# A four-layer hybrid decoder trunk: the first loads in two chains, and products of zeros ahead of the first weights

## What is computed

```python
proj = x @ w_in[l]                        # columns: xa, gb, gc (384 each), p (256), u, v (384 each)
ya = gb * causal_conv3(gc * xa)
yb = (trailing_mean(p) - p) @ w_pool * pool_scale
u, v = gelu(u), gelu(v)                   # v: normalised in heads of 64
yc = u * (w_spatial_masked @ v + b_spatial)          # in chunks of 128 tokens
h = layer_norm(ALPHA * x + concat(ya, yb, yc) @ w_o)
x = layer_norm(ALPHA * h + (silu(h @ w_gate) * (h @ w_up)) @ w_down)
```

## Time and profile before

| | |
|---|---|
| time, median of 3 runs (lowest to highest) | 2626.9 us (2626.42 to 2627.59) |
| time of the profiled execution | 2631.07 us |
| its span on the slowest core (core 4) | 2629.5 us |
| spans of the eight cores in it | 2619.5 to 2629.5 us |
| PE busy | 2547.4 us, 97% |
| DVE, ACT, POOL busy | 1328.5, 745.0, 400.4 us |

### The profile page before, as it was taken

The page is one execution under the profiler, slowest core; times in us unless marked ns, Lnnn a source line. Parts: engine busy times, 40 slices in busy tenths (PEclk is TensorE's granted clock), DMA queues, the critical chain, the costliest instruction groups (busy, mean ns, idle before and its releaser), DMA issues.

```text
span 2629.5 us, 36557 instructions; the slowest of 8 cores (2619.5 to 2629.5 us)
## 1 busy us (share of the span) xinstructions
PE 2547.4 (97%) x12080; PEld 1175.1 (45%) x12320; DVE 1328.5 (51%) x2441; ACT 745.0 (28%) x1273; POOL 400.4 (15%) x673
## 2 busy tenths in 40 slices
PE   6999999999999999999999999999999999999996
PEld 3444444444444444444444444444444444444443
DVE  5775332226887523133687752313468774322347
ACT  5533201013553410101365341010235433011022
POOL 4410000001441000000144100000014310000001
PEclk9999999999999999999999999999999999999998
DMA  7633423124364342212446343320354542332212
GB/s 175 134 65 69 76 32 68 25 46 70 60 106 73 61 84 51 40 17 50 79 70 103 54 81 65 59 34 15 59 83 77 97 77 45 64 57 34 37 42 96
DMA packets 161783, 173.02 MB, mean 66 GB/s; under 512 B 125120, under 2 KB 127296, under 8 KB 161600
## 3 DMA queue, kind: packets, MB, share of 16 engines
q0 software_dynamic: 32960, 113.39, 25.8%
q1 hardware_dynamic: 128640, 57.28, 10.4%
HBM read 246.27 MB, written 8.39 MB: 97 GB/s over the span
## 4 chain that ended last, share of the span: by engine, by line
PE 90%; issue 3%; DVE 2%; DMA 2%; POOL 2%; ACT 1%; DVEq 0%; POOLq 0%; ACTq 0%; SPq 0%
PE P L673 45%; PE P L689 23%; PE P L502 11%; PE P L659 8%; PE P L517 2%; DMA XT<-XB 1%; POOL SM L532 1%; DMA W<-w_chunks 0%; ACT VN L545 0%; PE P L558 0%; POOL T L612 0%; DMA X<-x 0%; DMA W<-w_v 0%; POOL SM L531 0%; DVE X L474 0%
## 5 line engine op out<-in xcount | busy, mean ns | idle before, releaser
L673 PE MATMUL P<-XT,W 128*128 128x512 bf16 x5517 | 1212.8, 379 | 6.1
L673 PEld LDWEIGHTS P<-XT,W 128*128 128x128 bf16 x5632 | 551.0, 98 | 664.6
L678 DVE TENSOR_TENSOR BIG<-P,T 128x512 bf16<-128x512 f32 x352 | 242.8, 690 | 766.9 <-PE P L673 708.3
L677 ACT ACTIVATE T<-P 128x512 f32<-128x512 f32 x352 | 209.5, 595 | 1247.7 <-PE P L673 1247.6
L689 PE MATMUL P<-W,BIG 128*128 128x512 bf16 x2257 | 515.9, 379 | 2.5
L485 DVE SCALAR_TENSOR_TENSOR X<-X,P 128x512 f32<-128x512 f32 x512 | 347.9, 686 | 334.4 <-PE P L689 292.9
L502 PE MATMUL P<-XT,W 128*128 128x512 bf16 x1745 | 406.8, 385 | 26.9 <-DVE T L625 14.6
L689 PEld LDWEIGHTS P<-W,BIG 128*128 128x128 bf16 x2304 | 225.4, 98 | 271.9
L502 PEld LDWEIGHTS P<-XT,W 128*128 128x128 bf16 x1792 | 174.4, 99 | 236.0 <-issue 40.9
L659 PE MATMUL P<-W,BIG 128*128 128x512 bf16 x1003 | 222.4, 379 | 1.2 <-ACT T L573 0.2
L478 POOL TENSOR_TENSOR MVB<-MVB,CNH 128x1 f32<-128x1 f32 x128 | 85.9, 671 | 761.8 <-DVE MVB L476 460.4
(11 more groups left out here) (65 smaller groups left out, 1096.6 us busy)
## 6 DMA issues: line engine op xcount, KB each, us to landing
W<-w_gu_t POOLq DMA_DIRECT2D x88, 512.0 KB, 6.3
W<-w_chunks POOLq DMA_DIRECT2D x56, 512.0 KB, 7.0
W<-w_dn_t POOLq DMA_DIRECT2D x36, 512.0 KB, 5.6
X<-x SPq DMA_DIRECT2D x16, 512.0 KB, 7.8
W<-w_o_t POOLq DMA_DIRECT2D x16, 512.0 KB, 6.4
out<-X SPq DMA_DIRECT2D x16, 512.0 KB, 2.6
W<-w_v POOLq DMA_DIRECT2D x16, 384.0 KB, 8.3
GBUF<-ln_g SPq DMA_DIRECT2D x8, 512.0 KB, 5.9
```

Source lines behind the costliest of these rows:

```text
L673: r = e.matmul(o.handle[:], lhsT=wv[:, h, k, :], rhs=XT[:, k, n * 512:(n + 1) * 512], start=(k == 0), stop=(k == 7))
L677: S.add("act", lambda e: e.activation(out=t.handle[:, 0:512], in_=pg.handle[:], func=AF.Silu), reads=[pg], writes=[t], dur=0.6, table="silu")
L678: S.add("dve", lambda e: e.tensor_tensor(out=BIG[:, ml, n * 512:(n + 1) * 512], in0=pu.handle[:], in1=t.handle[:, 0:512], op=ALU.mult), re ...
```

## The change

The opening list is taken apart. Token tiles and weights now form two chains: a tile waits for the tile three before it (x1 and x2 for x0), a weight load for the one two before it (c0 waits for x1, c1 for v1). The tiles are tied in order on SP by `heir` and `follow`, and the planner counts 524288 bytes for one instead of 786432. In the list the tiles stand earlier among the weights. The small parameters move from the front to behind x7 and wait until tile 3 stands in `XT`; the three constants PINV, PINVW and FLAG keep their place early on SP. A new function `heat` gives PE 5 and then 8 matmuls of 512 columns on a zeroed buffer, which stand ahead of everything else on PE. A new class G of PSUM banks (up to 4) takes the `gb` chunks and the sgu products out of class A.

```diff
-        S.pool("PS", [ps(f"P{b}", [128, 512]) for b in range(8)], {"A": 6, "F": 4, "T": 2})
+        S.pool("PS", [ps(f"P{b}", [128, 512]) for b in range(8)], {"A": 6, "G": 4, "F": 4, "T": 2})
...
-                o = S.vt("PS", "A")
+                o = S.vt("PS", "G" if c[0] == "gb" else "A")
...
-                m = S.vt("PS", "A")
+                m = S.vt("PS", "G")
...
+        def heat(src, n):
+            o = S.vt("PS", "T")
+
+            def mm(e):
+                for _ in range(n):
+                    r = e.matmul(o.handle[:], lhsT=src.handle[:, 0:128], rhs=src.handle[:, 0:512], start=True, stop=True)
+                return r
+
+            S.add("pe", mm, reads=[src], writes=[o], dur=n * 0.43)
...
-        order = "x0 v0 v1 x1 x2 x3 c0 c1 x4 x5 c2 x6 c3 x7 c4 c5 x8 c6 x9 x10 x11 x12 x13 x14 x15".split()
-        for k, what in enumerate(order):
+        order = "x0 v0 v1 x1 x2 x3 c0 x4 x5 c1 x6 x7 c2 x8 x9 c3 x10 x11 c4 x12 x13 c5 x14 x15 c6".split()
+        behind = {"x1": "x0", "x2": "x0", "x3": "x1", "c0": "x1", "c1": "v1"}
+        for i in range(4, NT):
+            behind[f"x{i}"] = f"x{i - 3}"
+        for i in range(2, 7):
+            behind[f"c{i}"] = f"c{i - 2}"
+        junk = S.vt("J")
+        S.add("dve", lambda e: e.memset(junk.handle[:], 0.0), writes=[junk], dur=0.6)
+        heat(junk, 5)
+        prev = None
+        for what in order:
             kind, i = what[0], int(what[1:])
-            after, mark = [("LD", k - 3)] if k > 2 else [], [("LD", k)]
+            after, mark = [("LD", behind[what])] if what in behind else [], [("LD", what)]
             if kind == "x":
-                sp_load(lambda i=i: X[:, i, :], x_d[i * 128:(i + 1) * 128, :], [("X", i), ("X", i, 0), ("X", i, 1)] + mark, 786432, reads=after)
+                o = sp_load(lambda i=i: X[:, i, :], x_d[i * 128:(i + 1) * 128, :], [("X", i), ("X", i, 0), ("X", i, 1)] + mark, 524288, reads=after)
+                if prev is not None:
+                    prev.heir, o.follow = o, True
+                prev = o
                 cast_transpose(i, "dve")
+                if i == 0:
+                    heat(junk, 8)
...
             if what == "x7":
-                load_small(l0)
+                load_small(l0, [("XT", 3)])
```

More of the change, by code:

```diff
@@ L742, in build_program @@
                 pre[1][i] = wload(w_c_d[l0, i], after=after, mark=mark)
[L743 to L746, removed]
+            if what == "x4":
+                sp_load(lambda: PINV[:], c_pinv_d, ["PINV"], prio=o.prio + 1)
+                sp_load(lambda: PINVW[:], c_pinvw_d, ["PINVW"], prio=o.prio + 1)
+                sp_load(lambda: FLAG[:], c_flag_d, ["FLAG"], prio=o.prio + 1)
             if what == "x7":
-                load_small(l0)
+                load_small(l0, [("XT", 3)])
         for li, l in enumerate(layers):
```

## The result

The changed kernel took 2633.34 us (median of 20 runs, from 2630.63), the kernel before 2627.51 on the same chip: a ratio of 1.0021, 95% interval 1.0014 to 1.0029. It is slower, by some 5.8 us. The forecast was 2624.9 us with a range of 2618.5 to 2631.5, and a chance of 0.14 for slower: the direction was wrong, and the time lies outside the range. The profiled execution took 2634.54 us; its slowest core is core 3 with 2633.0, where it was core 4 with 2629.5 before.

What follows compares the result with a forecast made beforehand. The prediction took PE to bound the kernel, with idle time to win in the opening. Gains of 3 us (opening) and 1 (banks), less 2 (tile 15), took the median of 2626.9 to 2624.9 us; range 2618.5 to 2631.5.

Steps and rivals of the forecast that it cites:

- The small parameters: Opening: moved behind x7 they land near 43 us, for products that come after 40 us; taken as 0.
- My condition: Opening: if the small parameters' move is not free, the first L628 waits, with all of PE behind it.
- The new class of banks: Half 1 of layer 0: chunks run further ahead and shorten PE's stall; gain 1 us, ends 0 and 3.
- Layer 0's stall in half 1: Layer 0: PE stood 4.53 us before; with 13.2 us of work in between it waits 1.1 us there, and more behind.
- tile 15: Layers 1 to 3: its cast on ACT comes 3.6 us late behind a gelu; cost 0 to 4.8 us, taken as 2.
- The opening: Up to about 60 us: earlier tiles and first chunk near 27 us give a lead of 3 us, ends 0 and +5.
- the tenth chunk: Opening: it ends near 58.5 us, where before it ended at 59.8 with three transposed tiles fewer.
- PE's idle time from 13 to 60 us: Sign in the changed kernel's profile: down by 3 us, with what is left ended by casts.
- the lower end of 0: Opening: a lead below 0 was ruled out, as no load is issued later except the small ones.
- the slower rival: Layers 1 to 3: late transposes of tile 15 bound each layer, with the slow clock behind; 2635.3 us, chance 0.14.
- The products of zeros: Start on PE: 5.6 us of matmuls delay nothing, first v tile still 2.72 us; taken as 0, ends 0 and +1.
- The stall on `T L625` in layers 1 to 3: First halves of layers 1 to 3: PE's order there does not change, so the wait stays near 4.7 us.

Runs made afterwards that it cites:

- e8: Changed kernel with the small parameters loaded at their old places, which also changed PE's order; 2627.7 us, ratio 1.0001 to the kernel before.
- e10: Changed kernel with small parameters at their old places and the bank class in layer 0 alone; 2626.4 us, ratio 0.9992 to the kernel before.
- e2: Changed kernel without the products of zeros (memset and two heat calls), all other order the same; 2632.8 us, ratio 1.0028 to the kernel before.
- e4: Changed kernel with POOL's issue of weight tile c3 moved behind the two powers (L532); 2632.8 us, ratio 1.0015 to the kernel before.
- e7: Changed kernel with the new bank class kept in layer 0 alone, removed from layers 1 to 3; 2632.1 us, ratio 1.0026 to the kernel before.
- e9: Changed kernel with four small-parameter loads issued early on SP, right behind x4, other engines' order kept; 2634.1 us, ratio 1.0032 to the kernel before.
- e1: Kernel before with the new bank class alone (sgu_out and gb chunks); 2628.9 us, ratio 1.0003 to the kernel before.
- e3: Kernel before with the 13 products of zeros alone; 2627.8 us, ratio 0.9998 to the kernel before.
- e5: Kernel before with spare products in four idle stretches of PE (17 in layer 0, 20 in each of layers 1 to 3); 2619.2 us, ratio 0.9969.

## Why the prediction was wrong

**The small parameters ("taken as 0").** This is the step that failed with the largest price: 4 to 5 us. Layer 0 took 217.3 and 218.1 us without their move (e8, e10) and 221.5 to 223.4 with it (after, e2, e4, e7, e9), and the cores' mean spans differ by 4 to 5 us in both pairs (after and e8, e7 and e10). I priced the landings, and did not price that the planner, told of a wait for XT tile 3, orders PE and DVE anew. My condition, that the first L628 waits, did not even occur. What that order brought is a wait of 3.2 to 3.6 us on `T L625` behind 24 sgu products on every core, with half speed behind it. It stayed when four of the loads came early (e9); how much of the 4 us it is stays open, since x5 came late in that run.

**The new class of banks ("a gain of 1 us").** Wrong in sign. Layer 0's stall in half 1 did shrink as predicted, to 3.6 us on all cores from 4.5 (4.0 to 4.3 on the others). The class alone does not do that: in e1 it is 4.0 to 4.3 us. I said that the order of the first halves of layers 1 to 3 does not change, and it did not; but I priced nothing in their second halves except tile 15. The class costs 2 to 3 us in layers 1 to 3 (e1, e7) and 1 to 2.3 in the cores' whole spans: a wait of 1.2 us in layer 2, a longer stall in layer 3 (5.06 for 4.65 us), and deeper falls of the clock. Why layer 3's stall is 0.4 us longer behind an order that is the same there, I did not find out.

**The opening (+3, ends 0 and +5).** The tiles came as computed, within 3 us: on core 3 x3 20.1, x4 22.1, x5 28.9, x6 33.3, x8 46.7, x10 51.1 us (predicted 20, 24.5, 29, 34, 46, 54), and the first chunk at 27.9 (27); in the mean of the eight cores it came 1.0 us earlier than before. The weights came 6 to 7 us later, c0 at 27.3 and c1 at 33.1 (21, 26). The rate was higher than I let it be, 215 to 248 against 197 GB/s. But the tenth chunk, forecast to end near 58.5 us, ended at 68.9 on core 3 (59.2 before on that core), and PE's idle time from 13 to 60 us rose by 2.3 us in the mean where it was to fall by 3. The step that failed is the one from landings to PE, and with it the lower end of 0, for which I gave only that no load is issued later: I counted tiles and took each as used 1.3 us after it lands. A tile has to pass DVE's order, that waits for POOL, and POOL waits for a weight tile (e4). And I counted waits at their length only. I had read in the earlier trace rows that products behind a stall take 0.46 us each, and used it in the heat and in the slower rival alone, not for the opening. With another order the pair of chains is worth about 1 us (e10 less e3), in the lower part of the bounds. The 1.00 of the earlier trace rows for the clock of the first stage, which I showed beside v tiles of 2.72 and 2.76 us, was no full speed either.

**The products of zeros (0).** Right within 1 us: e2 is level with the changed kernel, e3 is 0.9 us below the kernel before in the cores' mean spans, and the first v tile takes 2.71 us as predicted.

**Tile 15 (cost 2).** Wrong. The cast did move behind the gelu, and the transpose was issued at 762.62 in layer 1 of core 3; it landed 5.0 us later, at 767.6, and PE came to it at 768.95, so it did not wait. No core waited 2.5 us or more for a transpose in the changed kernel. The slower rival was on the right side of no change by luck: its mechanism did not occur, and at 2635.3 it named a time near the 2633.3 measured.

**The stall on `T L625` in layers 1 to 3 ("unchanged near 4.7").** Right within 0.4 us, and the missed chance: it was in the first view that I read, at 14.6 us, and its second half, the slow clock behind it, is worth more than the 2 us that I expected of the whole change: filled, the four stalls gave 8.0 us (e5).

## What to carry to other kernels

Where a planner sets the order, an edit of a wait or a buffer limit is priced by the two orders side by side, in each stage that repeats: here a load moved "for nothing" cost 4 to 5 us and a bank limit 1 to 2.3. PE's waits of 4.6 to 5.1 us cost once more by the clock behind them, 1.3 to 2.9 us for 16 products; where the wait can't be removed, spare products with operands that are ready, written into the bank that the next group overwrites, gave 0.24 to 0.34% in this kernel, in three different orders. And before a load's wait is put on an engine that also computes, look at what stands behind it there: one landing of c1 held POOL, then DVE, then a tile that had landed long before.

## What the runs showed of the hardware that I had not expected

The clock behind one and the same stall of 4.6 us was 0.83 in one layer and 0.68 in the next (and 0.83 or 0.66 after the change), which makes one layer 1.3 us longer on one core than on another, in both kernels; which of the two comes varies by core and layer. Heating PE and then letting it stand for 4.6 us, as the change does, left the first v tile at 2.71 us, as without heat. A granted clock of 1.00 at the start of the view can mean that there is no record yet: it stood beside eight products in 2.72 us that take 1.46 at the fast clock. The transfers of a core reached 234 to 262 GB/s over 20 us (40 to 60 us, eight cores), where the earlier trace rows had 197 with full queues.
